# The last 128 tokens' expert outputs: gathered rows summed on VectorE instead of matmuls

## The reference: what is computed

```python
def block(tb):                                    # 128 tokens
    qry = (tb @ w_q).reshape(PEER_BLOCK, PEER_HEADS, 2, PEER_HALF)
    s = jnp.einsum('thpd,pkd->thpk', qry, sub_keys)
    sv, si = lax.top_k(s, PEER_TOPK)
    ...                                           # 16 x 16 candidates, best 16 per head
    gates = jax.nn.softmax(top.astype(jnp.float32), axis=-1)
    z = jnp.einsum('thed,td->the', expert_u[eidx], tb)
    act = (gates * jax.nn.gelu(z.astype(jnp.float32))).astype(tb.dtype)
    return jnp.einsum('the,thed->td', act, expert_v[eidx])
```

## Time and profile before

| | |
|---|---|
| runs | 5169.2, 5170.85, 5170.98 us |
| profiled execution, span from first to last instruction | 5169.2 us |
| PE busy | 5120.1 us, 99% |
| DVE busy | 2913.2 us, 56% |
| ACT busy | 1349.7 us, 26% |
| POOL busy | 371.3 us, 7% |
| DMA, mean over the span | 123 GB/s |
| granted TensorE clock | 0.997 |

### The profile page before, as it was taken

The page is one execution under the profiler, slowest core; times in us unless marked ns, Lnnn a source line. Parts: engine busy times, 40 slices in busy tenths (PEclk is TensorE's granted clock), DMA queues, the critical chain, the costliest instruction groups (busy, mean ns, idle before and its releaser), DMA issues.

```text
span 5169.2 us, 68035 instructions
## 1 busy us (share of the span) xinstructions
PE 5120.1 (99%) x24691; PEld 4219.7 (82%) x24691; DVE 2913.2 (56%) x4428; ACT 1349.7 (26%) x1351; POOL 371.3 (7%) x512
## 2 busy tenths in 40 slices
PE   8999999999999999999999999999999999999998
PEld 6888889999988888778888888888888888888886
DVE  5555557666674334887888886222344444444443
ACT  4222222222233122122333333222222222222222
POOL 1111100000011011110000000000000000000002
PEclk9999999999999999999999999999999999999999
DMA  3222222222233334233344344433444343343422
GB/s 122 90 77 86 81 77 106 101 104 103 101 115 119 120 114 142 73 111 114 137 161 156 136 158 193 147 119 121 152 152 157 127 155 130 137 154 123 162 91 87
DMA packets 102293, 635.13 MB, mean 123 GB/s; under 512 B 11808, under 2 KB 12192, under 8 KB 44128
## 3 DMA queue, kind: packets, MB, share of 16 engines
q1 hardware_dynamic: 67152, 500.06, 26.8%
q0 software_dynamic: 35088, 134.37, 7.3%
HBM read 550.36 MB, written 83.95 MB: 123 GB/s over the span
## 4 chain that ended last, share of the span: by engine, by line
PE 95%; DVE 3%; issue 1%; POOL 0%; DVEq 0%; ACT 0%; DMA 0%; SPq 0%; POOLq 0%; ACTq 0%
PE bank L548 30%; PE bank L549 30%; PE bank L550 30%; PE bank L760 1%; PE bank L648 1%; PE bank L655 1%; PE bank L624 1%; POOL cand L497 0%; DVE w_lo L1152 0%; PE bank L646 0%; DVE s_rest L1473 0%; DVE si L1472 0%; DVE r L1663 0%; DVE cand_pos L1485 0%; DVE si L1485 0%
## 5 line engine op out<-in xcount | busy, mean ns | idle before, releaser
L548 PE MATMUL bank<-x_hi,w_hi 128*128 128x512 f32 (+1 forms) x7808 | 2886.8, 370 | 5.6 <-DVE w_lo L1152 5.6
L549 PE MATMUL bank<-x_lo,w_hi 128*128 128x512 f32 (+1 forms) x7808 | 2888.4, 370 | 0.0
L550 PE MATMUL bank<-x_hi,w_lo 128*128 128x512 f32 (+1 forms) x7808 | 2878.1, 369 | 0.0
L548 PEld LDWEIGHTS bank<-x_hi,w_hi 128*128 128x128 f32 x7808 | 1468.0, 188 | 293.0 <-issue 20.6
L549 PEld LDWEIGHTS bank<-x_lo,w_hi 128*128 128x128 f32 x7808 | 1466.9, 188 | 261.2 <-issue 2.6
L550 PEld LDWEIGHTS bank<-x_hi,w_lo 128*128 128x128 f32 x7808 | 1469.4, 188 | 257.1
L805 ACT ACTIVATE w_hi<-w_raw 128x2048 fp32r<-128x2048 f32 x432 | 827.5, 1916 | 2476.9 <-PE bank L550 2466.7
L1152 DVE TENSOR_TENSOR w_lo<-w_raw,w_hi 128x2048 fp32r<-128x2048 f32 x432 | 995.6, 2305 | 545.8 <-ACT w_hi L805 542.9
L1644 DVE TENSOR_TENSOR r<-bank,r 128x512 f32<-128x512 f32 x256 | 165.0, 686 | 632.3 <-PE bank L550 632.3
L1520 DVE TENSOR_TENSOR z_stage<-bank,rstd_b 128x512 f32<-128x512 f32 x128 | 88.5, 692 | 354.1 <-PE bank L550 350.6
L1314 DVE SCALAR_TENSOR_TENSOR r<-glu,conv_w,r 128x512 f32 (+1 forms) x240 | 178.9, 745 | 0.0
(11 more groups left out here) (238 smaller groups left out, 1858.0 us busy)
## 6 DMA issues: line engine op xcount, KB each, us to landing
w_raw<-u_blocks SPq DMA_DIRECT2D x128, 1024.0 KB, 4.8
w_raw<-v_blocks SPq DMA_DIRECT2D x128, 1024.0 KB, 4.8
w_raw<-w_proj SPq DMA_DIRECT2D x112, 1024.0 KB, 4.7
z_scratch<-z_stage POOLq DMA_DIRECT2D x128, 256.0 KB, 2.3
g_scratch<-g_chunk SPq DMA_DIRECT2D x8, 4096.0 KB, 12.3
z_group<-z_scratch POOLq DMA_DIRECT2D x16, 2048.0 KB, 9.9
g_group<-g_scratch POOLq DMA_DIRECT2D x16, 2048.0 KB, 16.9
w_raw<-w_mo SPq DMA_DIRECT2D x16, 1024.0 KB, 4.7
```

The costliest lines, as they stand in the source:

```text
L548: pe.matmul(dst, whi, xhi, start=start, stop=False)
L549: pe.matmul(dst, whi, xlo, start=False, stop=False)
L550: return pe.matmul(dst, wlo, xhi, start=False, stop=stop)
```

## The change

All 512 tokens still go through the Z stage. After it, the last 128 tokens (tile 3) leave the dense path:

- `TG = TT - 1`, `NT = 384`: gates, one-hots, products and output matmuls cover 384 tokens. `Z_GATE` is 48 in place of 64, still with 8 tokens per block. The output matmuls have 384 columns in place of 512, and so have `product`, `act_hi`, `product_lo` and the adds from PSUM.
- Right after routing VectorE computes, for the 128 tokens (on partitions) and their 128 pairs, the row number in `v_blocks` (`VI`) and in `z_scratch` (`ZI`), and keeps the gates (`GS`): ten small operations.
- POOL fetches. Once the last Z block has been multiplied it issues, for pairs 0 to 2, `v_row`; then for each of the 128 pairs one indirect DMA of one z per token (`ZP`, 4 bytes on each of 128 partitions); then `v_row` for the pairs 3 to 127. As `v_blocks` keeps an expert's row in eight pieces of 256 elements, one `v_row` is eight indirect DMAs of 128 rows of 1 KB. Three buffers of 128x2048 (`VG`) take the rows; `v_row(p)` waits until pair p-3 was added.
- VectorE adds, 128 times, `acc = VG * GS[:, p] + acc` (128x2048, tokens on partitions). `acc` lies in the last 128 columns of `R2`. The adds are spread over slots 16 to 119 of the output stage (80 slots with one, 24 with two), at the end of the slot. The first waits for all of `ZP`.
- After block 121 TensorE transposes `acc` (16 transposes of 128x128, four banks), and VectorE adds the result to the reloaded `h` rows (`HG`) in four operations of 512 columns.
- The group loads of groups 2 to 15 move from POOL to SyncE, behind the weight load of slot 3 of the group two before, at 1.5 MB each; groups 0 and 1 stay on POOL. The squares at the end are issued in another order over the last slots (`OUT_SQUARES`).

```diff
-Z_LOOK, Z_GATE = 16, 64
-TOK = T // Z_GATE
+Z_LOOK, Z_GATE, TOK = 16, 48, 8
+TG = TT - 1
+NT = TG * P
+VSLOT = 3
+V_FIRST, V_LAST = 16, 119
+OUT_SQUARES = [[], [], [], [0, 1, 2, 3], [4, 5, 6, 7], [8, 9], [10, 11], [12, 13]]
...
+            def out_blocks(gg, par, more):                                    # SyncE
+                for r in range(8):
+                    n = 16 * gg + (8 * par + r)
+                    sp.wait_ge(w_lo, n + (O1 + 1))
+                    sp.dma_start(RAW[r % 2][:, :], v_blocks[ds(n, 1), :, :].rearrange("o p n -> (o p) n")
+                                 ).then_inc(w_loaded[r % 2], 16)
+                    if more and r == 3:
+                        sp.wait_ge(x_lo, 16 * gg + (8 * par + 88))
+                        group_load(sp, 2 * gg + (par + 2), par, zg_ld, gg_ld)
...
+            def v_row(p):                                                      # POOL
+                for d in range(D // 256):
+                    pool.indirect_dma_start(VG[p % VSLOT][:, 256 * d:256 * d + 256], None,
+                                            v_blocks.rearrange("b i (j c) -> (b i j) c", j=GJ),
+                                            bass.IndirectOffsetOnAxis(ap=VI[:, p:p + 1], axis=0),
+                                            element_offset=P * D * d).then_inc(vg_ld[p % VSLOT], 16)
+            pool.wait_ge(ix_rdy, 3)
+            pool.wait_ge(w_used, O1 + 2)
+            for p in range(VSLOT):
+                v_row(p)
+            z_flat = z_dram.rearrange("j i t -> (j i t)").unsqueeze(1)
+            for p in range(P):
+                pool.indirect_dma_start(ZP[:, p:p + 1], None, z_flat, bass.IndirectOffsetOnAxis(ap=ZI[:, p:p + 1], axis=0)
+                                        ).then_inc(zp_ld, 16)
+            for p in range(VSLOT, P):
+                pool.wait_ge(vg_use, p - VSLOT + 2)
+                v_row(p)
...
+            for r in range(8):                                                 # TensorE, last group
+                out_block(120 + r, r % 2, 1)
+                if r == 1:
+                    pe.wait_ge(vg_use, P + 1)
+                    for q in range(4):
+                        for k in range(4):
+                            m = pe.transpose(A[1 + q][:, P * k:P * k + P], acc[:, 4 * q + k, :], ident[:])
+                        m.then_inc(at_rdy, 1)
...
+            def v_add(p):                                                      # VectorE
+                if p == 0:
+                    dve.wait_ge(zp_ld, 16 * P)
+                    link(dve.tensor_tensor(GS[:, :], GS[:, :], ZP[:, :], ALU.mult))
+                dve.wait_ge(vg_ld[p % VSLOT], 128 * (p // VSLOT) + 128)
+                dve.wait_ge(vg_use, p + 1)
+                dve.scalar_tensor_tensor(acc, acc3(VG[p % VSLOT]), GS[:, p:p + 1], acc, ALU.mult, ALU.add).then_inc(vg_use, 1)
+            def v_due(n):
+                at_ = lambda m: min(max(m - V_FIRST, 0) * P // (V_LAST + 1 - V_FIRST), P)
+                return range(at_(n), at_(n + 1))
+            for g in range(KEYS // GJ):
+                par, more, tail = g % 2, g < KEYS // GJ - 1, g == KEYS // GJ - 1
                 for r in range(8):
...
-                        dve.tensor_tensor(R2[:, 2 * r + k, :], o_bank[r % 2][k][:, :], R2[:, 2 * r + k, :], ALU.add
-                                          ).then_inc(evac_v, 1)
+                        o = R2[:, 2 * r + k, 0:NT]
+                        dve.tensor_tensor(o, o_bank[r % 2][k][:, 0:NT], o, ALU.add).then_inc(evac_v, 1)
...
                     for jj in NEXT_TILES[r] if more else []:
-                        product(1 - par, jj, 16 * gg + 16 if par == 0 else 16 * gg + 32)
-                        product_lo(1 - par, jj, 16 * gg + (80 + 8 * par + 8))
+                        product(g + 1, 1 - par, jj)
+                        product_lo(1 - par, jj, 8 * g + 88)
+                    for p in v_due(n):
+                        v_add(p)
```

More of the change, by code:

```diff
@@ L277, in encoder_block @@
         zg_ld = [sem("z_group_loaded0"), sem("z_group_loaded1")]
+        gg_first = [sem("g_group_first0"), sem("g_group_first1")]
+        zg_first = [sem("z_group_first0"), sem("z_group_first1")]
         act_rdy = sem("act_ready")
+        ix_rdy = sem("pair_indices_ready")
+        zp_ld = sem("z_pairs_loaded")
+        vg_ld = [sem(f"v_row_loaded{s}") for s in range(VSLOT)]
+        vg_use = sem("v_row_added")
+        hg_ld = sem("h_rows_loaded")
+        at_rdy, at_add = sem("v_sums_turned"), sem("v_sums_added")
         v_root = sem("final_root_ready")
@@ L322, in _ @@
                 z_load(2 * i)
-            with sp.Fori(0, T // CH // 2) as cc:
+            with sp.Fori(0, NT // CH // 2) as cc:
                 for half in range(2):
@@ L330, in _ @@
             for s in range(2):
-                sp.wait_ge(g_st[s], 8 * (T // CH) + 16)
+                sp.wait_ge(g_st[s], 8 * (NT // CH) + 16)
             sp.wait_ge(h_st, 16)
-            sp.dma_start(R2[:, :, :], h_dram.rearrange("p (k t) -> p k t", k=KT)).then_inc(o_ld, 16)
+            h3 = h_dram.rearrange("p (k t) -> p k t", k=KT)
+            sp.dma_start(R2[:, :, 0:NT], h3[:, :, 0:NT]).then_inc(o_ld, 16)
+            for s in range(2):
+                sp.dma_start(HG[s][:, :, :], h3[:, 8 * s:8 * s + 8, NT:T]).then_inc(hg_ld, 16)
             with sp.Fori(0, (NB_E - Z_LOOK - 4 - Z_GATE) // 2) as i:
                 z_load(Z_LOOK + 4 + Z_GATE + 2 * i)
-            stream(v_blocks, NB_E, O1)
+            def out_blocks(gg, par, more):
[7 more added lines that the diff above has]
+                        group_load(sp, 2 * gg + (par + 2), par, zg_ld, gg_ld)
+            with sp.Fori(0, 7) as gg:
+                for par in range(2):
+                    out_blocks(gg, par, True)
+            for par in range(2):
+                out_blocks(7, par, False)
             for k in OUT_ORDER:
@@ L524, in _ @@
                 pool.wait_ge(z_st[s], 8 * NB_E)
[L526 to L531, removed]
+            group_load(pool, 1, 1, zg_first, gg_first)
+            def v_row(p):
[15 more added lines that the diff above has]
+                v_row(p)
             pool.wait_ge(x_lo, 80 + 8 * 15)
@@ L747, in _ @@
             for k, src in enumerate((EI, EJ, GA)):
-                for t in range(TT):
+                for t in range(TG):
                     m = pe.transpose(A[k][:, P * t:P * t + P], src[:, t, :], ident[:])
@@ L772, in _, with out_block @@
             pe.wait_ge(g_add, 4 * Z_GATE + 4)
-            with pe.Fori(0, KEYS // GJ // 2) as gg:
-                for par in range(2):
[L775 to L789, removed]
+            def out_block(n, u, par):
+                pe.wait_ge(w_lo, n + (O1 + 3))
+                pe.wait_ge(evac_v, 2 * n + (120 - 2))
+                for k in range(2):
+                    if (u, k) == (1, 1):
+                        pe.wait_ge(z_out, NB_E)
+                    for jj in range(GJ):
+                        wcol = slice(jj * 256 + k * P, jj * 256 + k * P + P)
+                        m = mm3(o_bank[u][k][:, 0:NT], WH[u][:, wcol], WL[u][:, wcol],
+                                XHO[:, GJ * par + jj, :], XLO[:, GJ * par + jj, :], jj == 0, jj == GJ - 1)
+                m.then_inc(w_used, 1)
@@ new lines, in out_group @@
+            def out_group(gg, par):
+                pe.wait_ge(x_lo, 80 + 8 * par + 8 + 16 * gg)
+                pe.sem_inc(turns[2], 1)
+                with pe.Fori(0, 4) as m_:
+                    for u in range(2):
+                        out_block(16 * gg + 8 * par + 2 * m_ + u, u, par)
+            with pe.Fori(0, KEYS // GJ // 2 - 1) as gg:
+                for par in range(2):
+                    out_group(gg, par)
+            out_group(7, 0)
+            pe.wait_ge(x_lo, 80 + KEYS)
@@ L1049, in _ @@
             act.wait_ge(tr_rdy, 3)
[L1050 removed]
+            act.activation(AH[:, :], A[2][:, 0:NT], ACT.Copy).then_inc(tr_ah, 1)
             act.wait_ge(tr_ah, 1)
             act.wait_ge(h_st, 16)
[L1053 removed]
+            with act.Fori(0, NT // CH // 2) as cc:
                 for half in range(2):
@@ L1091, in ogroup @@
                     u = r % 2
-                    if tail and r >= 1:
-                        out_square(2 * r - 2)
-                        out_square(2 * r - 1)
+                    for k in OUT_SQUARES[r] if tail else []:
+                        out_square(k)
                     act.wait_ge(w_used, 16 * gg + (b + 3))
@@ L1590, in _ @@
             dve.sem_inc(g_add, 4)
-            with dve.Fori(0, T // CH // 2) as cc:
+            with dve.Fori(0, NT // CH // 2) as cc:
                 for half in range(2):
@@ L1637, in _ @@
             dve.wait_ge(o_ld, 16)
-            def ogroup(gg, par, more, tail):
+            dve.memset(acc, 0.0).then_inc(vg_use, 1)
+            acc3 = lambda t: t[:, :].rearrange("p (k d) -> p k d", k=KT)
+            def v_add(p):
[5 more added lines that the diff above has]
```

(9 more changed lines are left out.)

92 lines of the change are left out of this document (61 added, 31 removed).

## The result

The changed kernel takes 5685.03 us (median of 4 runs, 5683.37 to 5688.65) against 5170.61 us before: ratio 1.0996, 95% interval [1.0981, 1.1012]. It is 514 us slower; the forecast was 4942 and the range 4800 to 5400.

What follows compares the result with a forecast made beforehand. TensorE was taken to bound the kernel before, POOL's indirect DMAs after: 3790 + 1152 x 1.0 us = 4942 us, where 3790 is the Z stage's end at 3706.9 plus 83.2 after the last fetch. Range 4800 to 5400.

Steps and rivals of the forecast that it cites:

- t: Time from one indirect DMA to the next on POOL, taken as 1.0 us, between 0.83 and 1.18.
- POOL's part decides: POOL's 1152 indirect DMAs, from the Z stage's end, set the kernel's end: 4942 us at 1.0 us each.
- the issue's own time: On POOL, an indirect DMA without waiting: 0.54 us direct plus 0.29 for reading indices, 0.83 us.
- the waits: POOL's issues held off by VectorE operations: up to 11.65 us per slot, 1.18 us per issue; the middle was taken.
- the prediction's line: Kernel end as 3790 us plus 1152 times the time per indirect DMA on POOL; passes 5169 at 1.20 us.
- PE alone: If TensorE sets the output stage's pace with 384 columns, 0.1744 us per matmul: 4805 us.
- VectorE's part: Output-stage slots of 7.9 to 8.6 us against PE's 8.37, row add 2.35 us: just fits, 0 us taken.
- 3790 + 1152 t: Kernel end in us if POOL's indirect DMAs set the pace; 4942 at 1.0 us per DMA.
- Rival 3: POOL's queue, 3707 to slot 119: indirect issues cost over 1.2 us, kernel slower, 5289 us; chance 0.38.
- The rule of the Trainium skill: A two-SBUF-input VectorE instruction and a GpSimd instruction reading SBUF contend; the second blocks until the first is done.
- DMA's part: Output-stage slots move 2.6 MB in 8.4 us, 312 GB/s: fits, 0 us taken, 25 if only 306 come.
- even at twice: An output-stage weight load needs 4.8 us to land and is in time even at double that.

Runs made afterwards that it cites:

- e3_narrow: The changed kernel with all fetches kept, but VectorE's row add covering 128 of 2048 channels; sums incomplete: 5449.71 us.
- e4_psum: The changed kernel with the running sum of the rows in four PSUM banks, so a row add has one SBUF input: 5472.23 us.
- e6_nofetch: The changed kernel without indirect DMAs and row adds (last 128 tokens get only h): 4805.8 us.
- e7_two_late: The changed kernel with a second, row-by-row weight copy for one 8 KB-per-row fetch per pair, adds in slots 26 to 120: 4821.63 us.
- e5_rows: The changed kernel with weights laid out row by row, one 8 KB fetch per row, weight blocks loaded in 1 KB pieces: 4960.75 us.
- e5b_rows_late: As e5_rows, but the row adds begin at slot 26 and end with slot 120: 4930.54 us.

## Why the prediction was wrong

**The step that failed** is the choice of t in "POOL's part decides": 1.0 us, from 0.83 without waiting and 1.18 with. It was 1.64, which over 1152 issues is 735 us more. Two terms of it were mis-sized: the issue's own time by 0.43 us (495 us), and the waits, for which 0.17 us per issue or 196 us were put in and which came to 419 (223 us). Some 17 us are single longer gaps and one wait for a buffer.

- The issue's own time. I took 0.54 (a direct DMA) + 0.29 (a small operation that reads SBUF) = 0.83; it is 0.96 and a gap of 0.30 before the next, 1.26. The gap had no counterpart in the rows I used: a direct DMA follows another without one (in the kernel before one starts at 3727.13 and takes 0.90 us, the next starts at 3728.03). By the prediction's line 1.26 alone gives 3790 + 1152 x 1.26 = 5242 us, slower than before. This is worked out, not run.
- The waiting. I let about one issue through per VectorE operation and got 0.35 us per issue at the top; measured, 1.341 - 0.957 = 0.38 us on a row piece, 394 us in all (e3_narrow and e4_psum take 0.21 to 0.23 us of it away) and 25 more on the fetches of z. I then took the middle between this and no waiting. That was the poorer choice: the earlier trace rows showed the wait in full, and no row spoke for an indirect DMA that escapes it. The even 540 ns of the earlier trace rows are of direct DMAs, which read no indices.

**Right**: PE alone. 4805 us were forecast against the span, and the span of e6_nofetch is 4804.3, with 0.173 us per matmul for 0.1744. That it met so closely is in part luck: two small errors cancel. The prediction took TensorE's matmul at 3722.99 for one of the last of the Z stage, but VectorE scales the last z block, which it waits for, at 3721.10, so the Z stage ended some 2 us earlier; in e6_nofetch the first matmul of 384 columns starts at 3703.98 and in the changed kernel at 3704.75, not at 3706.9. In return the output stage of e6_nofetch took 1075.5 us, transposes included, for 1073.4. VectorE's part: the row add 2.352 us for 2.35, `lo` 2.28, 384 columns 0.55; and VectorE just fits, as e7_two_late shows with 174.89 us busy in 200. The form of the sum, 3790 + 1152 t, holds within 7 us. The transposes took 1.91 us in e6_nofetch at a granted clock of 1.00, as forecast (2), and 3.68 us in the changed kernel, where TensorE had stood idle for 13.01 us before them and the clock was 0.50.

**Rival 3**, with its place in POOL's queue, its sign and its point of decision at 1.20, is what happened; its price of 5289 was too low for the same two reasons. In the forecast's own words it was wrong if "the mean of an indirect DMA with its gap" came "above 1.2 us, longer beside `lo` and the row adds than elsewhere": 1.65, and 1.54 for the fetches of z, where no row adds run.

The rule of the Trainium skill ("SBUF — State Buffer", "Who interferes with whom") holds for the indirect DMA on Trainium2 as far as these runs go: held behind two-input operations (2.22 to 2.83 us for 0.96), free again when the second input moved to PSUM. I had named it as speaking against the change and then priced it at half.

**DMA's part** was not put to the test by the changed kernel, whose slots took so long that it moved 166 GB/s from 4000 to 5600 us, far below the 312 forecast. e7_two_late tested it and it held: 341 GB/s at a share of 0.90, with PE at 99%. My remark that pieces of 1 KB may do worse came true in e5_rows, on SyncE's side of it. That a weight load would be in time "even at twice" 4.8 us did not hold: in e5b_rows_late it took 9.7 us, and ScalarE waited 270.5 us for raw weights.

## What to carry to other kernels

Count the issues of an indirect DMA before its bytes: here 128 rows of 128 bytes, of 1 KB and of 8 KB all cost GpSimd about the same (medians of 0.952, 0.957 and 0.947 to 0.951 us), so the layout should make one fetch of one row, even by a second copy of the weights. When a queue moves to an engine that shares something with a busy one, price it by the held case in the trace and not by a middle. Before such a change, run it without the new work (as e6_nofetch): that bounds the gain in one run, and the price per issue can be read from any small kernel that has one. Its waits cannot: they depend on what VectorE does beside it, here 419 us for 1152 issues and 399 us for 640.

## What the runs showed of the hardware that I had not expected

- The gap of 0.30 us before every indirect DMA on GpSimd, in all variants with one (311.6 us over 1023). It belongs to the indirect DMA that comes: it stands between the last direct DMA and the first `v_row`, too, and not behind the last `v_row` (5599.82, 0.96 us), after which a memset starts at 5600.78. Direct DMAs in the same kernel follow each other without it.
- The fetches of 4 bytes cost 1.151 us each beside 1.341 for 1 KB, and among their gaps are five longer ones of 2.2 to 5.3 us (50.2 us over 128). What causes those is open.
- A block of 1 MB loaded by SyncE in 1 KB pieces took 9.0 to 9.7 us to land beside the row fetches, against 4.8 in 8 KB pieces in the kernel before, and the two kernels that differ in it, e5b_rows_late and e7_two_late, lie 109 us apart. The landing in e7_two_late is not in its profile; ScalarE's wait for raw weights fell from 270.5 to 51.2 us.
- In the changed kernel TensorE, which waits for weights in most slots, has a mean granted clock of 0.80 to 0.83 in the windows from 4000 us on (1.00 in e6_nofetch, where it is busy throughout). The mean is made of two levels. After 5.40 us idle its matmuls of 384 columns start 0.32 us apart at a clock of 0.50 (1.2 GHz, 4401.0 to 4405.5), then 0.17 us apart at 1.00 (2.4 GHz, 4406.3 to 4411.3). TensorE is not on the path in those slots. It is on it at the transposes, where the lower level cost 1.8 us.
